# A fourth landing slot for streamed weights, with on-chip room found by overlays

## The reference

```python
for l in range(DEPTH):                      # first block, DEPTH = 2
    h = rmsnorm(x, norm_g[l])
    proj = h @ w_in[l]                      # split into q, k, v, gates, index parts, mix
    ...                                     # ya (causal), yb (selected keys), ym (memory)
    up = einsum('bsnw,nwd->bsnd', stack(ya, yb, ym), w_branch[l])
    x = x + sum(sigmoid(mix) * up) @ w_out[l]
x = rmsnorm(x, final_g)
```

```python
for l in range(DEPTH):                      # second block, DEPTH = 2
    h = x @ w_in_2[l]
    mix = concat([gla(h), rwkv7(h), nsa(h)]) @ w_out_2[l]
    x = layer_norm(ALPHA * x + mix)
    ffn = (silu(x @ w_gate[l]) * (x @ w_up[l])) @ w_down[l]
    x = layer_norm(ALPHA * x + ffn)
```

## Time and profile before

| what | value |
|---|---|
| time, median of 3 runs | 1549.4 us (1549.4 to 1552.5) |
| time of the profiled execution | 1543.15 us |
| its span, first to last instruction | 1541.6 us |
| TensorE busy | 1495.2 us, 97% |
| GpSimd busy | 961.6 us, 62% |
| ScalarE busy | 779.3 us, 51% |
| VectorE busy | 701.9 us, 46% |
| read from memory | 225.58 MB |

### The profile page before, as it was taken

One profiled execution on the slowest core, in us unless ns is written; L12 is line 12 of the kernel. 1 busy time (PEld: TensorE's weight loads), 2 busy tenths in 40 slices (PEclk: granted clock), 3 DMA queues, 4 the chain that ended last, 5 costly groups with the idle time before them and its releaser, 6 DMA issues. The chain is left out here.

```text
span 1541.6 us, 20723 instructions
## 1 busy us (share of the span) xinstructions
PE 1495.2 (97%) x7896; PEld 1232.6 (80%) x7896; DVE 701.9 (46%) x1092; ACT 779.3 (51%) x1232; POOL 961.6 (62%) x416
## 2 busy tenths in 40 slices
PE   7999999999999999999999999999999999899997
PEld 6888788878887888788788768888788797688886
DVE  3222865472137762645665851110347667612112
ACT  5544665445445665358444444443477344454342
POOL 6887538888885468877200278878774002488785
PEclk9999999999999999999999999999999999999999
DMA  7666326555664346565311157655553311366563
GB/s 237 170 184 178 110 84 177 173 173 164 195 178 123 110 124 221 178 189 151 118 56 56 55 151 221 188 156 193 168 161 111 110 56 55 109 178 182 147 199 128
DMA packets 121633, 227.97 MB, mean 148 GB/s; under 512 B 10304, under 2 KB 26176, under 8 KB 121536
## 3 DMA queue, kind: packets, MB, share of 16 engines
q1 hardware_dynamic: 120384, 222.46, 48.3%
q10 hardware_dynamic: 1152, 4.19, 0.9%
HBM read 225.58 MB, written 1.05 MB: 147 GB/s over the span
## 5 line engine op out<-in xcount | busy, mean ns | idle before, releaser
L179 POOL TENSOR_TENSOR parts<-raw,parts 128x1024 fp32r<-128x1024 f32 (+5 forms) x412 | 961.4, 2346 | 565.5 <-ACT parts L172 563.3
L210 PE MATMUL ps<-parts,xT 128*128 128x512 f32 (+4 forms) x2624 | 810.2, 386 | 9.6 <-ACT H L715 3.0
L172 ACT CAST parts<-raw 128x1024 fp32r<-128x1024 f32 (+5 forms) x412 | 416.0, 1012 | 430.1 <-PE ps L210 252.7
L210 PEld LDWEIGHTS ps<-parts,xT 128*128 128x128 f32 x2624 | 487.2, 188 | 114.1 <-issue 5.2
L210 PE MATMUL ps<-parts,x_low 128*128 128x512 f32 (+3 forms) x672 | 251.2, 382 | 0.0
L210 PE MATMUL ps<-parts,M_low 128*128 128x512 f32 (+2 forms) x640 | 244.3, 386 | 0.0
L210 PEld LDWEIGHTS ps<-parts,x_low 128*128 128x128 f32 x672 | 126.7, 189 | 22.9 <-issue 0.5
L210 PEld LDWEIGHTS ps<-parts,M_low 128*128 128x128 f32 x640 | 120.4, 188 | 20.3
L210 PE MATMUL ps<-parts,aT 128*128 128x512 f32 x352 | 109.8, 395 | 0.6 <-POOL parts L179 0.6
L210 PE MATMUL ps<-parts,H_low 128*128 128x512 f32 x272 | 106.0, 394 | 0.0
L210 PEld LDWEIGHTS ps<-parts,aT 128*128 128x128 f32 x352 | 66.0, 187 | 16.7 <-POOL parts L179 1.1
(11 more groups left out here) (351 smaller groups left out, 1802.3 us busy)
## 6 DMA issues: line engine op xcount, KB each, us to landing
raw<-in_w_in SPq DMA_DIRECT2D x160, 512.0 KB, 3.6
raw<-in_ffn_w_down SPq DMA_DIRECT2D x44, 512.0 KB, 4.5
raw<-in_ffn_w_gate SPq DMA_DIRECT2D x40, 512.0 KB, 3.7
raw<-in_ffn_w_up SPq DMA_DIRECT2D x40, 512.0 KB, 3.7
raw<-in_w_out SPq DMA_DIRECT2D x32, 512.0 KB, 3.5
raw<-in_w_branch SPq DMA_DIRECT2D x24, 512.0 KB, 3.4
raw<-in_w_mem_kv SPq DMA_DIRECT2D x16, 512.0 KB, 3.5
raw<-in_w_in SPq DMA_DIRECT2D x16, 366.0 KB, 3.2
```

The lines of the kernel that those rows point to most:

```text
L172: self.nc.scalar.copy(self.part(i, 0)[:, 0:nk, 0:w], self.raw(i)[:, 0:nk, 0:w]).then_inc(self.hi_ready.sem, 1)
L179: self.nc.gpsimd.tensor_tensor(self.part(i, 1)[:, 0:nk, 0:w], self.raw(i)[:, 0:nk, 0:w], self.part(i, 0)[:, 0:nk, 0:w], ALU.subtract).then ...
L210: ins = pe.matmul(b[:, 0:w], a(k0 + 2 * n + c, t), self.part(i, lo_w)[:, c, 0:w], start=(opens and n == p == 0), stop=(final and p == len( ...
```

## The change

The landing slots become four. The 4 KB of a partition that the fourth takes are found by laying buffers over others: in the first layers `acc` and `bbias` go into the key half of `KV`, and the rotation's scratch into the second half of `sm`; in the second layers `BP` and `SP[0]` go into the first four rows of `sw`, and VectorE waits, before it writes `BP`, until bank "mg" is read out. All else that is sized by `RAW` follows: one more landing semaphore, `load` waits for item i − 4, and at the very start `W.load(sp, RAW + 2)` issues six items ahead of x where it issued five.

```diff
-RAW = 3
+RAW = 4
@@ first layers
-        acc = sb("acc", [P, NT, S])
-        bbias = sb("bbias", [P, NT, S])
-        ra, rb = acc[:, :, :].rearrange("p t s -> p (t s)"), bbias[:, :, :].rearrange("p t s -> p (t s)")
+        acc, bbias = (KV[:, n, 0:HALF].rearrange("p (t s) -> p t s", t=NT) for n in range(2))
+        ra, rb = (sm[:, 1, 2 * n:2 * n + 2, :].rearrange("p a s -> p (a s)") for n in range(2))
@@ second layers
-        BP = sb("BP", [P, 2, S])
+        BP = sw[:, 0:2, :]
...
-        SP = [sb("SP", [P, 4, P]), LD[:, 2:4, :].rearrange("p a (b n) -> p (a b) n", b=2)]
+        SP = [sw[:, 2:4, :].rearrange("p a (b n) -> p (a b) n", b=2), LD[:, 2:4, :].rearrange("p a (b n) -> p (a b) n", b=2)]
...
+                TP.drained(dve, ("mg",))
                 tt(BP[:, :, :], BB[:, :, :], EN[:, :, :], ALU.mult, E("tilde"))
```

## The result

The changed kernel took **1537.88 us** (median of four executions, 1536.71 to 1538.75), the one before 1549.4 in the same measurement (1548.32 to 1552.5): a ratio of **0.9922 [0.9905, 0.9939]**, 11.5 us faster. I had forecast 1544.8, 4.6 us faster. The profiled execution took 1538.75 us for a span of 1537.3; the one read of before took 1543.15 for 1541.6. From profile to profile the gain is therefore 4.3 us of span, nearly the 4.6 of my sum; from median to median it is over twice that. That gap is what the experiments are about.

What follows compares the result with a forecast made beforehand. The prediction took TensorE as the bound, busy 1495.2 of 1541.6 us, with waits from late landings over three slots. Five gains summed to 4.6 us, costs taken as 0: 1544.8 us from 1549.4, range 1543.0 to 1546.4.

Steps and rivals of the forecast that it cites:

- which no row explains; I carry the difference over: Last step: the runs' median lay 6.3 us above the profiled execution less the gain; this was added unchanged, giving 1544.8 us.
- Terms 1 to 3: First layers, ends of narrow steps: TensorE's waits for a product's copy behind a late cast end; gains 1.54, 1.51, 0.43 us.
- Term 5: At 1098.03 us TensorE waits for xT from ScalarE, delayed by a cast's landing wait; gain 0.3 us, between 0 and 0.50.
- Term 4: Last item of the down projection, at 1090.26 us: TensorE's wait for a late subtraction ends; gain 0.79 us.
- The ring: Slot's round of load, cast, subtraction: 2.03 (narrow) and 2.73 us (down) an item with three slots, 1.52 and 2.05 with four.
- (a): Cost of laying index sums over the key half of `KV` and the rotation's scratch over `sm`: nothing, between −0.1 and +0.1.
- (b): Cost of VectorE waiting for bank "mg" before `BP`: 1.0 us later in layer 1, covered with 0.4 to spare; taken as 0.
- (c): Cost at the start of four loads going out before the first wait instead of three: at most 2.6 us, taken as 0.
- (d): Cost of a fourth load in flight on the DMA engines: nothing, since the average transfer rate stays 194 GB/s.
- A: Rival, chance 0.20: the waits are only half ended, each end of step still waits 0.7 us; 1547.1 us.
- B: Rival, chance 0.10: no effect, landings being late for want of transfer rate and not of slots; 1549.4 us.
- C: Rival: subtractions slide onto VectorE's chain from `BP` to rotated queries; slower, 1551.8 to 1555.0 us; chance 0.08 with small costs.

Runs made afterwards that it cites:

- experiment 1: The kernel before with three slots, run again with no edit: 1549.5 us, ratio 1.0 [0.999, 1.001].
- Experiment 2: The changed kernel with four slots, run again with no edit: 1538.86 us, ratio 0.9929 [0.9916, 0.9942] to the kernel before.
- experiment 6: The changed kernel, but loads wait as with three slots in the second layers' gate, up and down steps; 6.4 to 7.0 us slower than with four slots.
- experiment 9: The changed kernel, but loads wait as with three slots in the second layers' gate and up steps alone: 1542.52 us, ratio 0.9949 to the kernel before.
- experiment 7: The changed kernel, but loads wait as with three slots in steps 9, 10, 11 and 4 of the first layers; 2.8 to 3.3 us measured for them.
- experiment 5: The changed kernel, but loads wait as with three slots throughout the first (hybrid) layers; 3.3 to 3.7 us measured for them.
- experiment 11: The kernel before with three slots, but in steps 9 to 11 ScalarE copies tile 0 ahead of the cast: 1548.42 us, ratio 0.9986 [0.9974, 0.9998].
- experiment 10: The changed kernel, but loads wait as with three slots in the second layers' down projections alone: 1540.05 us, ratio 0.993 to the kernel before.
- experiment 3: The changed kernel with all overlays and the wait for bank "mg", but three slots: 1550.68 us, ratio 0.9998 to the kernel before.
- experiment 4: The changed kernel with its four places, but only three loads in flight: 1549.75 us, ratio 0.9999 [0.9988, 1.001] to the kernel before.

## Why the prediction was wrong

**Which step failed: "which no row explains; I carry the difference over".** What was wrong is the 6.3 us between the profiled execution and the median, taken for a constant that both kernels have. The kernel with four slots has no such offset: its two profiled executions took 1538.75 and 1536.67, on both sides of its median. In 77 timed executions of the kernel before, on several chips, none took less than 1545.16 us, and 1543.15 was read. I had treated a lucky execution as the kernel and its usual time as an offset. The luck had two parts, as experiment 1 shows: 2.9 us fewer stalls, which a fourth slot ends, and 3.5 us less time in TensorE's matmuls, at a granted clock of 0.993 that only one of the 73 executions with a recorded clock reached. (On which chip it was taken is not on record.)

**The sum was near for that execution, and nearer by luck.** The profile of the changed kernel is 4.3 us of span shorter, but at a clock of 0.991. Experiment 2 has the same TensorE time as the execution that I read (1495.3 against 1495.2), and its span is 6.5 us shorter, all of it idle time. Against the 4.6 of the sum, 0.7 for H L2184 and 0.7 for the first products of gate and up (xT L2134, 1.2 us before, 0.5 after) were not priced.

**The term that was mis-sized: the feed-forward.** The sum has 0.79 and 0.3 for it; experiment 6 measured 6.4 to 7.0 us, of which gate and up alone are 3.1 to 3.7 (experiment 9). For the down projection I had "2.73 an item, against 2.76: even, with nothing in hand", and then priced only the stalls that showed. For gate and up I had nothing at all. The same sum would not have shown it by itself: with their landings of 3.6 us it gives 2.43 an item, and the casts came every 2.41, so there 0.3 us an item are in hand. What they have besides is the gap of 3 us at the opening. Up to 2.44 an item it is made up far enough by the next end of a step; at 2.52 and above it is not. Three slots are just enough in the execution that I read, and not in the others.

**Terms 1 to 3** (1.54, 1.51, 0.43) held: their sum of 3.5 stands against 2.8 to 3.3 measured in experiment 7 and 3.3 to 3.7 in experiment 5 (with 3.1 us of interval), the stalls are gone after, and experiment 11 shows that the copy behind the cast is the link. TensorE's wait for this copy is 2.4 to 3.7 us in all six traces with three in flight there and the old order, so here one execution was enough. **Term 5** is 0.3, as taken. **Term 4** is gone as forecast in the profile, but its 0.79 was one draw: the idle time shown, 0.63 then, is 1.33 and 2.31 in experiments 10 and 6.

**The ring.** The sums gave 1.52 and 2.05 us an item for four slots, and ScalarE's waits for landings fell from 129.4 to 5.5 us. A fourth outstanding load did not stretch the landings there (3.6 us after, 4.5 before in the same steps), so the guard of a third was not needed. With the Trainium skill, DMA: Bandwidth & Descriptors, "Anatomy of one DMA", an estimate was 3.2 us for a landing, by which three slots are enough in the down projection. The trace does not agree: medians of 3.6 to 4.5 were measured, and with three in the down projection alone TensorE stalls 1.33 us at its end (experiment 10).

**The costs.** (a) and (b) at 0: right, experiment 3 has 0.9998 [0.9985, 1.0012] for both together, and the wait for bank "mg" puts `BP` off by 1.06 us under cover. That H L2184 would stay at 6.0 was wrong by 0.7 us to the good; at its long place in the first recurrent layer it has 1.83 us, where it had 2.18, and with three slots and the overlays 1.84. I have not found the link. (c) is not quite nothing: in the first 40 us a landing takes 4.8 us in the median and 9.6 at most in the profile after (4.3 and 7.3 in experiment 2), where before and experiments 1, 3 and 4 have 3.9 to 4.2 and at most 6.4 to 6.8, so my sign "no longer than 6 us" held for medians only. TensorE's wait for the memory is 8.0 and 6.3, against 6.4 and 6.5. (d) at 0: later than the start the landings are alike (3.5 to 3.7 us in the median).

**The rivals.** A fell: the copy does not cost 0.7 at each end but nothing. B fell: the landings were late for want of slots, by experiment 4 above all. C fell: GpSimd's sliding did not lengthen VectorE's chain, H L2184 shrank. The chances were also summed wrongly: the forecast's 0.62 less 0.04 is 0.58 for faster and not 0.60, and by the parts given "same" is 0.37 and "slower" 0.05, not 0.33 and 0.07.

**The clock's share.** It is small. The mean granted clock of the kernel before is 0.9903 over its executions and of four slots 0.9913. At one and the same clock, 0.991, the kernel before has a mean of 1549.4 us (22 executions, none below 1546.1) and four slots 1538.8 (7, none above 1539.3): 10.6 us. At 0.992 it is 1548.2 (10) and 1536.9 (3): 11.3 us. So some 10.6 of the 11.5 us are there without any difference of clock. Experiment 1 and the changed kernel's profile, both at 0.991, differ by 10.7 us of span. Within the kernel before the time goes with the clock all the same, at 1261 us for one unit (correlation 0.66), which is 1.3 us for the 0.001 between the kernels. Whether fewer stalls are what raises it was not tested.

**What is open.** Why the landings take longer in one execution than in another; why H L2184 shrank; and the sum of experiments 9 and 10 against 6.

## What to carry to other kernels

When a ring's round divided by its slots comes out near the consumer's period, don't price it by the stalls of one profile: it stalls or not by chance, and its mean over executions is the cost. Where there is something in hand, set it against the gap with which the stage opens and the number of items until the next end of a step. If the profiled execution is faster than every timed one, ask first what it had that the others lack, its granted clock among it; a difference "which no row explains" belongs in the sum as an unknown term that the change may take away, with its full size in the range. And read the reckoning for every step that shares the ring, not only for the one where the profile happens to show a wait.

## What the runs showed of the hardware

**Three slots scatter more than four.** The 77 timed executions of the kernel before have a standard deviation of 2.1 us around 1550.1, ten of four slots 1.0. The stalls at the ends of steps are one cause of it, falls of the clock another; how much each has was not separated.

**The time of a landing moves from execution to execution.** The 45 loads issued from 905 to 1033 us, gate and up and the first three of the down projection, minimum, median and maximum to landing: 2.7, 3.6 and 4.9 us in the execution read of before; here the same in experiment 1, the same program:

```profile
DMA to landing us min/median/max: 2.6/4.1/5.6
```

Half a microsecond on a round of 8 is 0.17 an item over three slots, more than the 0.03 that was in hand in the down projection, and most of what separates 2.41 from 2.65 us an item in gate and up.

**The clock may fall or not at one place.** At the opening of gate and up, four matmuls take 2.07 us in experiment 1, where the granted clock is 0.50 from 904 to 906, its lower level of 1.2 GHz:

```profile
903.39 2.07 PE L210 MATMUL ps<-parts,xT 128*128 128x512 f32 x4 [0.41 <-ACT xT L2134]
```

At the same place in the execution read of before they take 1.20 us at 1.00, after a wait of 0.34. Such a fall costs some 1.5 us until the clock is back: with four loads in flight, gate and up takes 132.4 to 132.7 us with one (experiments 5, 7 and 10) and 130.9 to 131.1 without.
